# Placing the last two experts' rows by 0/1 products in PSUM, and asking for the stored rows behind the 30th scatter

## What is computed

```python
def run_block(args):
    x_blk, e = args
    return (jax.nn.silu(x_blk @ w1[e]) * (x_blk @ w3[e])) @ w2[e]
...
yb = yb * buf_w[:, None].astype(yb.dtype)
out = jnp.zeros((n_tok + 1, d), yb.dtype).at[buf_tok].add(yb)[:n_tok]
```

## Time and profile before

| | |
|---|---|
| median of three runs | 1470.92 us |
| the profiled execution | 1472.18 us |
| its span, first to last instruction | 1470.4 us |
| granted TensorE clock, mean of the span | 0.98 |
| TensorE busy | 1325.5 us, 90% |
| VectorE, ScalarE, GpSimd busy | 36%, 28%, 27% |
| DMA, mean of the span | 206 GB/s |

### The profile page before, as it was taken

The page is one execution under the profiler, slowest core; times in us unless marked ns, Lnnn a source line. Parts: engine busy times, 40 slices in busy tenths (PEclk is TensorE's granted clock), DMA queues, the critical chain, the costliest instruction groups (busy, mean ns, idle before and its releaser), DMA issues. The chain is left out here.

```text
span 1470.4 us, 16826 instructions
## 1 busy us (share of the span) xinstructions
PE 1325.5 (90%) x6354; PEld 889.8 (61%) x6354; DVE 536.5 (36%) x1077; ACT 418.4 (28%) x814; POOL 390.7 (27%) x373
## 2 busy tenths in 40 slices
PE   6999998999999899987777887748999998999899
PEld 5677775898768633332222232317888887887566
DVE  3649957340242511111111111128311425464662
ACT  5333366263421100000000000016222224344641
POOL 7644223168310112211111111000445430000320
PEclk9999999999999999999999999988999999999999
DMA  7231222244405799999999999974323222221100
GB/s 211 62 113 58 70 103 81 90 145 144 172 33 208 309 415 421 418 422 421 421 424 422 422 423 422 422 306 149 115 86 114 86 86 86 87 88 56 58 22 36
DMA packets 74131, 302.52 MB, mean 206 GB/s; under 512 B 10392, under 2 KB 10440, under 8 KB 53328
## 3 DMA queue, kind: packets, MB, share of 16 engines
q1 hardware_dynamic: 66576, 286.99, 49.7%
q0 software_dynamic: 7488, 14.60, 3.1%
HBM read 295.26 MB, written 14.68 MB: 211 GB/s over the span
## 5 line engine op out<-in xcount | busy, mean ns | idle before, releaser
L774 POOL TENSOR_TENSOR ring_rounded<-ring,ring_rounded 128x512 fp32r<-128x512 f32 x192 | 252.2, 1350 | 345.0 <-ACT ring_rounded L1526 345.0
L902 PE MATMUL bank<-HT_rounded,ring_rounded 128*128 128x512 f32 (+1 forms) x576 | 221.2, 384 | 3.8 <-DVE ring_rounded L2452 1.9
L904 PE MATMUL bank<-HT_rounded,ring_rounded 128*128 128x512 f32 (+1 forms) x576 | 217.6, 378 | 0.0
L903 PE MATMUL bank<-ring_rounded 128*128 128x512 f32 (+1 forms) x576 | 217.4, 378 | 0.0
L1229 PE MATMUL bank<-ring,B 128*64 128x512 f32 x704 | 160.7, 602 | 27.0 <-DMA ring<-in_w 26.2
L904 PE MATMUL bank<-ring_rounded 128*128 128x512 f32 x352 | 139.0, 395 | 0.0
L1526 ACT ACTIVATE ring_rounded<-ring 128x2048 fp32r<-128x2048 f32 x54 | 103.0, 1914 | 115.0 <-DMA ring<-in_w_in_a 56.1
L902 PEld LDWEIGHTS bank<-HT_rounded,ring_rounded 128*128 128x128 f32 x576 | 108.4, 188 | 30.7 <-issue 5.9
L2343 DVE TENSOR_TENSOR B<-bank,small 128x512 f32<-128x512 f32 x32 | 22.1, 692 | 284.9 <-PE bank L1219 284.9
L1229 PEld LDWEIGHTS bank<-ring,B 128*64 128x64 f32 x704 | 49.2, 137 | 121.6 <-issue 86.3
L904 PEld LDWEIGHTS bank<-HT_rounded,ring_rounded 128*128 128x128 f32 x576 | 108.4, 188 | 20.3
(11 more groups left out here) (400 smaller groups left out, 1992.4 us busy)
## 6 DMA issues: line engine op xcount, KB each, us to landing
ring<-in_w SPq DMA_DIRECT2D x88, 1024.0 KB, 30.7
A<-in_w SPq DMA_DIRECT2D x20, 2048.0 KB, 33.1
ring<-in_w SPq DMA_DIRECT2D x11, 2048.0 KB, 33.3
HT<-in_w SPq DMA_DIRECT2D x20, 1024.0 KB, 32.9
XN<-in_w SPq DMA_DIRECT2D x20, 1024.0 KB, 29.6
ring<-in_w_in_a SPq DMA_DIRECT2D x16, 1024.0 KB, 5.1
ring<-in_w_in SPq DMA_DIRECT2D x14, 1024.0 KB, 7.2
ring<-in_w_in_b SPq DMA_DIRECT2D x8, 1024.0 KB, 5.5
```

Source lines behind the costliest of these rows:

```text
L774: last = pool.tensor_tensor(r32(lo), lo, r32_read(quarter(g, True)[:, k, :]), ALU.subtract)
L902: pe.matmul(o, r32(a_hi), r32(b_hi), start=first, stop=False)
L903: pe.matmul(o, r32(a_hi), r32(b_lo), start=False, stop=False)
L904: return pe.matmul(o, r32(a_lo), r32(b_hi), start=False, stop=last)
```

## The change

Only 30 experts scatter their rows. The results of experts 30 and 31 stay in PSUM: `down_last` puts the first 512 columns of both into bank 6 and the second 512 into bank 7, one expert in each half of the partitions. VectorE scales bank 6 and ScalarE bank 7 into `y_last` (128 rows, 64 of each expert). VectorE also makes two tables of 0 and 1, `last_oh`, 128 rows by 512 tokens, with a 1 where the row belongs to the token; one of the two has the halves swapped, as the banks have. In `last_rows` TensorE then forms a tile in two banks: the two stored rows of each token, multiplied by the identity, and `last_oh` times `y_last`. `add_last` adds the bank to the residual rows, in place of `add_back`.

Since two experts no longer write to it, `y_dram` is filled with zeros in the first stage (four writes of 1 MB from a zeroed buffer), so that a token whose row was not scattered reads zero. SyncE asks for the norm vectors behind the 30th `down`, and for tiles 0 and 1 of `y_back` when 30 scatters have landed. The halves of c0 move behind these two tiles, and tiles 2 and 3, which now go to A1, stand behind c0 and the 31st `down`. The low parts of c0 are made by VectorE between the steps of tiles 0 and 1. Squares are written to A0, and overflow items use the first buffer set.

```diff
+        y_over = B2[:, 1536:2048]
+        y_last = E[:, 1024:2048]
+        last_scale, last_at, last_at2, blocks = B2[:, 160:162], B2[:, 162:164], B2[:, 164:166], B2[:, 168:176]
+        last_oh = [B2[:, 512:1024], B2[:, 1024:1536]]
...
-        y_back = [f3(XN if t < 2 else A0, (2, D), 2048 * (t % 2)) for t in range(NT)]
-        g_fin, g_a_row = B0[:, 0:D], B0[:, D:2 * D]
+        y_back = [f3(XN if t < 2 else A1, (2, D), 2048 * (t % 2)) for t in range(NT)]
+        g_fin, g_a_row = A0[:, 0:D], A0[:, D:2 * D]
+        x3_squares = f3(A0, (2, D), 2 * D)
...
+                    sp.wait_ge(sem("zeros_ready"), 1)
+                    for q in range(4):
+                        sp.dma_start(y_dram[SEQ * q:SEQ * q + SEQ, :].rearrange("(p r) n -> p r n", p=P),
+                                     y_over.unsqueeze(1).to_broadcast([P, 4, 512])).then_inc(sem("y_zeroed"), 16)
...
-
-            sp.wait_ge(h_done, EXPERTS - 1)
-            for h in range(2):
-                load_half(2 * chunk_no["c0"] + h)
+            sp.wait_ge(y_done, EXPERTS - 2)
+            sp.dma_start(g_fin, a["norm_final_g"].partition_broadcast(P)).then_inc(sem("g_fin_loaded"), 16)
+            sp.dma_start(g_a_row, a["ln_a_2"][0].partition_broadcast(P)).then_inc(sem("g_a_row_loaded"), 16)
...
 
             sp.wait_ge(sem("rows_stored"), 1)
-            sp.wait_ge(sem("pe_left_experts"), 1)
-            for t in range(NT):
+            for t in range(NT):
+                if t == 2:
+                    sp.wait_ge(h_done, EXPERTS - 1)
+                    for h in range(2):
+                        load_half(2 * chunk_no["c0"] + h)
+                    sp.wait_ge(y_done, EXPERTS - 1)
                 for c in range(2):
                     src = y_dram.rearrange("(h r) n -> r h n", h=2)[512 * c + P * t:512 * c + P * t + P]
                     sp.dma_start(y_back[t][:, c, :].rearrange("p (h n) -> p h n", h=2), src)\
                       .then_inc(sem(f"y_back{t}"), 16)
-                if t == 1:
-                    sp.dma_start(g_fin, a["norm_final_g"].partition_broadcast(P)).then_inc(sem("g_fin_loaded"), 16)
-                    sp.dma_start(g_a_row, a["ln_a_2"][0].partition_broadcast(P)).then_inc(sem("g_a_row_loaded"), 16)
             sp.wait_ge(h_done, EXPERTS)
...
-            for e in range(24, EXPERTS):
+            for e in range(24, PAIR):
                 step_rows(e, e)
             for b in range(2):
-                pool.wait_ge(sem(f"y_stored{b}"), 16 * EXPERTS // 2)
+                pool.wait_ge(sem(f"y_stored{b}"), 16 * PAIR // 2)
...
+            def down_last(j, n):
+
+                pe.wait_ge(sem("gT_ready"), PAIR + j + 1)
+                pe.wait_ge(we_loaded[n % 3][2], 16 * ((PAIR + j) // 3 + (n % 3 > 0)))
+                pe.wait_ge(sem("y_ready"), PAIR)
+                w = as_expert(w_slot[n % 3][2], 2).rearrange("p (k n) -> p k n", k=4)
+                for k in range(4):
+                    for hf in range(2):
+                        at = 64 * ((hf + j) % 2)
+                        last = pe.matmul(bank[6 + hf][at:at + 64, :], gT[n % 2][:, k, :],
+                                         w[:, k, 512 * hf:512 * hf + 512], start=(k == 0), stop=(k == 3),
+                                         skip_group_check=True)
+                last.then_inc(y_done, 1)
 
...
+            n_over = pe.value_load(over_n, min_val=0, max_val=OVER)
+            down_last(1, 7)
             pe.wait_ge(sem("y_ready"), EXPERTS)
-
...
+            pe.wait_ge(sem("y_last_ready"), 1)
...
+
+            def last_rows(t, outs):
+
+                pe.wait_ge(sem(f"y_back{t}"), 32)
+                for b, o in enumerate(outs):
+                    cs = slice(512 * b, 512 * b + 512)
+                    for c in range(2):
+                        pe.matmul(o[:, :], ident, y_back[t][:, c, cs], start=(c == 0), stop=False)
+                    pe.matmul(o[:, :], last_oh[b][:, P * t:P * t + P], y_last[:, cs], start=False, stop=True)\
...
                 for b in range(2):
                     o = fill(V, "x4_t", t, b)
-                    if t == 0 and b == 0:
-                        pe.wait_ge(sem("x3_ready"), 1)
-                        spin(o, 9)
+                    if t < 2 and b == 0:
+                        spin(o, 5)
                     pe.wait_ge(sem("x4n_ready"), t + 1)
                     for k in range(4):
                         last = pe.transpose(o[:, P * k:P * k + P], y_back[t][:, 0, 4 * b + k:D:KD], ident)
                     last.then_inc(bank_filled, 1)
 
+            for t in range(2):
+                last_rows(t, [fill(V, "last", t, b) for b in range(2)])
             turn_x4(0)
             turn_x4(1)
+            last_rows(2, [fill(V, "last", 2, b) for b in range(2)])
+            tile3 = [fill(V, "last", 3, b) for b in range(2)]
             outs = [fill(V, "c", j) for j in range(4)]
             part = chunk("c0")
-            spin(outs[0], 4)
             for h in range(2):
...
                         last.then_inc(bank_filled, 1)
-                    elif j % 2 == 1:
-                        turn_x4(2 + j // 2)
+                    elif j == 0:
+                        last_rows(3, tile3)
...
             act.wait_ge(sem("y_done"), EXPERTS)
+            act.wait_ge(sem("y_stored1"), 16 * PAIR // 2)
+            act.wait_ge(sem("last_oh_ready"), 2)
+            act.activation(y_last[:, 512:1024], bank[7][:, :], ACT.Copy, scale=last_scale[:, 1:2])\
...
 
             square_x3(0)
+            square_x3g(0)
             square_x3(1)
-            for t in range(2):
-                square_x3g(t)
-                roots(16 + 2 * t, 18 + 2 * t)
+            roots(16, 18)
+            high_half("c0", 0)
+            square_x3g(1)
+            roots(18, 20)
...
+
+            for b in range(2):
+                top, bottom = PAIR + b, PAIR + 1 - b
+                dve.tensor_copy(last_scale[0:SLOTS, b:b + 1], tab_w[0:SLOTS, top:top + 1])
+                dve.tensor_copy(last_scale[SLOTS:P, b:b + 1], tab_w[SLOTS:P, bottom:bottom + 1])
+                dve.tensor_copy(last_at[0:SLOTS, b:b + 1], tab_s[0:SLOTS, top:top + 1])
+                last = dve.tensor_copy(last_at[SLOTS:P, b:b + 1], tab_s[SLOTS:P, bottom:bottom + 1])
+            own(last)
+            own(dve.tensor_scalar(blocks, const("item_row")[:, 0:TILES], float(SLOTS), None, ALU.mult))
+            own(dve.tensor_tensor(last_at, last_at, const("half_col").to_broadcast([P, 2]), ALU.subtract))
+            dve.tensor_scalar(last_at2, last_at, -float(SEQ), None, ALU.add)
+            own(dve.tensor_tensor(f3(B2, (TILES, SLOTS), 1536),
+                                  const("slot_row")[:, 0:SLOTS].unsqueeze(1).to_broadcast([P, TILES, SLOTS]),
+                                  blocks.unsqueeze(2).to_broadcast([P, TILES, SLOTS]), ALU.add))
+            row_no = y_over
+            for b, oh in enumerate(last_oh):
+                own(dve.tensor_scalar(oh, row_no, last_at[:, b:b + 1], None, ALU.is_equal))
+                dve.scalar_tensor_tensor(oh, row_no, last_at2[:, b:b + 1], oh, ALU.is_equal, ALU.add)\
+                   .then_inc(sem("last_oh_ready"), 1)
+
+            step_gate(PAIR // 2, 1)
+            dve.wait_ge(sem("y_done"), EXPERTS)
+            for b in range(2):
+                dve.wait_ge(sem(f"y_stored{b}"), 16 * PAIR // 2)
+            dve.wait_ge(sem("last_oh_ready"), 2)
+            dve.tensor_scalar(y_last[:, 0:512], bank[6][:, :], last_scale[:, 0:1], None, ALU.mult).then_inc(sem("y_ready"), 2)
...
-            def add_back(t):
+            def add_last(t):
 
                 dve.wait_ge(sem("x_home"), 16 * NT)
-                dve.wait_ge(sem(f"y_back{t}"), 32)
-                own(dve.tensor_tensor(x_rows[:, t, :], x_rows[:, t, :], y_back[t][:, 0, :], ALU.add))
-                dve.tensor_tensor(x_rows[:, t, :], x_rows[:, t, :], y_back[t][:, 1, :], ALU.add)\
-                   .then_inc(sem("x3_ready"), 1)
+                for b in range(2):
+                    o = filled(V["last", t, b])
+                    v = x_rows[:, t, 512 * b:512 * b + 512]
...
-            for step, t in ((add_back, 0), (add_back, 1), (scale_final, 0), (scale_final, 1), (normalise_x4, 0),
-                            (normalise_x4, 1), (add_back, 2), (low_x4, 0), (low_x4, 1), (scale_final, 2),
-                            (add_back, 3), (normalise_x4, 2), (scale_final, 3), (normalise_x4, 3), (low_x4, 2),
-                            (low_x4, 3)):
+            low_c0 = lambda h: low_half("c0", h)
+            for step, t in ((add_last, 0), (scale_final, 0), (add_last, 1), (normalise_x4, 0), (scale_final, 1),
+                            (low_c0, 0), (normalise_x4, 1), (low_c0, 1), (low_x4, 0), (low_x4, 1),
+                            (add_last, 2), (scale_final, 2), (add_last, 3), (normalise_x4, 2), (scale_final, 3),
+                            (normalise_x4, 3), (low_x4, 2), (low_x4, 3)):
                 step(t)
             ss_total[0] += 2 * NT
```

(15 more changed lines are left out.)

74 lines of the change are left out of this document (43 added, 31 removed).

## The result

The changed kernel takes 1482.73 us (median of 5 runs, 1477.55 to 1484.31), the kernel before 1470.69 (median of 5 runs beside it, 1469.27 to 1474.62). The ratio is 1.0062, with a 95% interval from 1.0048 to 1.0077: slower by 7 to 11 us. The two medians by themselves lie 12.0 us apart, more than this interval holds; with five runs each, spread over 6.8 and 5.4 us, I go by the ratio. The forecast was 1480.6 us and a range of 1472 to 1485. The profiled execution took 1482.73 us with a span of 1480.4.

The account below looks back on a forecast made before the run. TensorE, busy for 90% of the span, bounds the kernel. First c0 product +4.1, tile 3's products +5.2, a wait -0.4, cooling +0.8 sum to +9.7 us: median 1480.6 us, range 1472 to 1485.

Parts of the forecast that it names:

- first product of c0, against before: At the seam, TensorE's first product with c0 moves from 1008.46 to 1012.6 us, behind tile 2's products: +4.1 us.
- stage of c0, against before: Within c0's stage, tile 3's products add 5.2 us and a wait of 0.40 us goes.
- second stretch at the low clock: Before tile 2's products TensorE may cool again; 3.1 us at half speed cost 1.6, taken as 0.8 us.
- The landing: Tile 0's stored rows land at 984.7 us, behind residual rows and norm vectors, 6.9 us earlier; bounds 979.3 and 987.3.
- rival A: Stored rows land beside the residual rows by 980.1 us and TensorE never cools: +2.0, 1472.9 us; chance 0.12.
- The low clock at the head: Clock falls 2.0 us into TensorE's idle time, so tile 0's products run their first 3.1 us at half speed.
- The price: A full-precision product of 512 columns costs TensorE 0.87 us, six per tile 5.2 us, four tiles 20.9 us.
- B: A product on TensorE costs half, 0.44 us: about +1, 1472.0 us; chance 0.04.
- C: Early landing beside the residual rows and half-price products together: -6.7, 1464.2 us, the only way to faster; chance 0.08.
- The chain: From landing through products, adds and norm steps, tile 0 is turned at 1000.4 us against 1001.46; 1.1 of 6.9 us left.
- What was priced at nothing: 0/1 tables in VectorE's idle stretch, two scatters fewer, adds from PSUM, first-stage zeros (bounds 0 to +3 us), filler: 0 us.
- D: Worse: tile 0 lands at 987.3 (+2.6), a cold tile 2 (+0.8 more), 3 us from the zeros: 1487 us; chance 0.06.

Follow-up runs that it names:

- e3: Changed kernel with the two norm vectors requested behind tile 1's stored rows, not ahead of tile 0's; ratio to the kernel before 1.0041, seam 62.6 us.
- e2: Changed kernel with tile 3's six products, inside the first pass of c0, issued twice; one run, 1488.04 us, seam 74.4 us.
- e6: Changed kernel with tile 0's six products, at the head of the chain, issued twice; one run, 1486.02 us, seam 73.1 us.
- e1: Changed kernel with stored rows added on VectorE, no such products on TensorE, rows of experts 30 and 31 left out; ratio to before 0.9971, seam 55.4 us.
- e9: Kernel before with only the zeros added, four DMAs writing 4 MB to y_dram; ratio to the kernel before 0.9996 (0.9982 to 1.0011).
- e4: Changed kernel with only the 0/1 products on TensorE, GpSimd adding the stored rows of tiles 1 to 3; ratio to before 1.0014, seam 62.2 us.

## Why the prediction was right

Times are counted from the end of `down`, since the stages ahead moved by 1.3 us:

| step | forecast | measured |
|---|---|---|
| tile 0 of the stored rows there | +6.6 | +6.5 |
| at half clock after that | 3.1 us | 3.0 us |
| tile 0's, tile 1's products done | +13.3, +18.5 | +13.2, +18.3 |
| turn of tile 0 | +22.3 | +22.1 |
| tile 1 turned | +29.3 | +28.6 |
| first product of c0, against before | +4.1 us | +3.0 us |
| stage of c0, against before | +4.8 us | +4.8 us |
| second stretch at the low clock | +0.8 us | none |
| sum | +9.7 us | +7.8 us in the seam, +10.0 in the span |

*The landing.* The choice of 984.7 between 979.3 and 987.3 decided whether the loss would be one that can be told; the earliest landing alone (rival A) still gave +2.0, so the sign did not hang on it. The queue did hand out data about in the order of requests. The norm vectors, asked for at 959.33 and 959.71, landed (KB, us from issue to landing)

```profile
A<-in_norm_final_g SPq DMA_DIRECT2D x1, 512.0 KB, 22.6
A<-in_ln_a SPq DMA_DIRECT2D x1, 512.0 KB, 23.4
```

that is at 981.9 and 983.1, and tile 0, asked for from 969.98, at 985.8, 2.7 us behind the second. e3, which takes 1 MB out of the way, moves the landing by the 2.6 us of these bytes. Whether the slowest of the sixteen engines set this landing no run separates from the bytes; their mean share was 0.99 and 1.05 in the two windows from 982 to 986.

*The low clock at the head.* That it lasts 3.1 us from the first product was right for this profile, and partly luck: with the same instructions ahead it lasted 5.0 us in e2 and 5.5 in e6, which costs 1.0 to 1.2 us more. Nor does the clock fall 2.0 us into an idle time each time, as the prediction takes from rows 10: in the changed kernel it was still up 2.6 us in (1.00 in 980 to 982), in e1 and e6 it fell about 5 us in (0.70 and 0.73 in 984 to 986), and in e3 not within 3.90.

*The price.* Six products take 5.2 us (tile 1's, from 992.56 to 997.71 at full clock), as rows 9 said. The Trainium skill's price (TensorE: Matmul & The Clock Gate, "Back-to-back issue gap": 131 ns for 512 columns in a sustained stream), times the four passes that the prediction counts, would make 3.1, an estimate; the measurement decides, and e1 shows what hangs on it: 11.3 us of the seam. Rivals B and C fell with it.

*The chain.* That the landing's gain would be eaten before the first turn was right: of 7.0 us (13.5 and 6.5 behind `down`), 1.3 are left at the turn of tile 0 (+23.4 before, +22.1 now). Three small terms were too large. VectorE came to the end of tile 1's norm 0.5 us earlier than summed and the turn took 1.0 for 1.1; and the first record of c0 stands 4.75 us behind tile 2's first and not 5.2, because records of neighbouring products overlap: together 1.1 us. And I had allowed for a second fall of the clock at half its price; it didn't fall. Scatter outside the seam of +2.2 us put the profiled span back onto the forecast, so its agreement to 0.3 us (10.0 and 9.7) is partly luck. By the ratio the change costs 9.1 us, 7.1 to 11.3, which holds both 7.8 and 9.7; the measured median lies 2.1 us above the forecast 1480.6.

*What was priced at nothing.* The zeros: at most 0.11% in e9, and no more than 0.4 us at 210 us of its timeline. The 0/1 tables: they lie in 960.0 to 965.0 with 4.9 us of idle time behind them, ahead of the last gate.

*Rivals.* A asked for a landing 2.0 us behind `down`; e3's 3.9 is the earliest seen. Its condition for a warm TensorE was too strict, since e3 stayed warm at 3.9. D's landing (+9.2) and zeros did not come, its cold tile 2 did in e2 (+1.5).

## What to carry to other kernels

Ask for each part of a replaced step on which engine it was free. Here the round trip through memory cost only idle time, the early requests and the new order were worth 3.5 us together, and moving all adds onto TensorE, which is the bound, cost 11.3; the split that keeps on TensorE only what needs a product, or what falls in a hole, turned 1.0062 into 0.9966. When a transfer is requested earlier, count the bytes queued ahead of it: its own request may go out 16 us earlier (970.0 for 986.2) and its data land only 7 us earlier.

## What was not expected of the hardware

- GpSimd and VectorE hold each other up on float32 tensor-tensor steps in SBUF: a 128x1024 step of VectorE took 3.02 us for 1.28, a step of one column 1.93 for 0.16, a GpSimd add 4.27 for 2.35. Giving GpSimd a share cost 3.7 us of the seam against giving it none (2.9 us by the two ratios, whose intervals overlap; e4 also had one root a step earlier).
- The granted clock is not the same from one execution to the next for the same instructions: ahead of tile 2's products it stayed at 1.00 in the changed kernel and fell in e2, a difference of 1.5 us, and at the head of the chain it rose 3.0, 5.0 and 5.5 us after the first product in the changed kernel, e2 and e6. A chain with such waits on TensorE has this scatter built in.
- In e3's profile an earlier landing paid twice: 2.6 us by itself and 1.5 because TensorE, idle for 3.90 us and not for 6.46, was still at 2.4 GHz.
